# VectorE's weight splits moved ahead of the S5 set-up in the first mixer of a two-layer decoder trunk

## What is computed

```python
for l in range(DEPTH):                       # 2 layers, 256 tokens, width 1024
    h = rms_norm(x, mix_norm[l])
    z = h @ w_in[l]                          # 1024 -> 5632 columns
    u, q, k, v, g_ssm, g_attn = jnp.split(z, SPLITS, axis=-1)
    y_a = s5_branch(u, ...)                  # diagonal complex state space model, 32 groups x 64 states
    y_a = jax.nn.gelu(y_a)
    y_a = y_a * jax.nn.sigmoid(y_a @ w_glu[l] + b_glu[l])
    q, k = apply_rope(q), apply_rope(k)      # per 64-wide component
    y_b = diff_attention(q, k, v, lam)       # 8 heads, two maps each, then a norm per head
    m = sigmoid(g_ssm) * (y_a @ w_proj_ssm[l]) + sigmoid(g_attn) * (y_b @ w_proj_attn[l])
    x = x + m @ w_out[l]
    x = x + FFN(rms_norm(x, ffn_norm[l]))    # layer 0 dense, layer 1 top-2 of 8 experts
return rms_norm(x, final_norm)
```

## Time and profile before

| what | value |
|---|---|
| median of three runs | 1532.93 us |
| the profiled execution | 1532.64 us, of which the span of the trace is 1530.9 us |
| TensorE busy in the span | 1489.4 us (97%) |
| VectorE, ScalarE, GpSimd busy | 1214.7, 901.7 and 72.8 us |
| bytes moved by DMA | 393.07 MB, mean 257 GB/s |
| mean granted TensorE clock | 0.992 of full speed |

### The profile page before, as it was taken

One profiled execution on the slowest core, in us unless ns is written; L12 is line 12 of the kernel. 1 busy time (PEld: TensorE's weight loads), 2 busy tenths in 40 slices (PEclk: granted clock), 3 DMA queues, 4 the chain that ended last, 5 costly groups with the idle time before them and its releaser, 6 DMA issues.

```text
span 1530.9 us, 23739 instructions
## 1 busy us (share of the span) xinstructions
PE 1489.4 (97%) x8995; PEld 1262.2 (82%) x8995; DVE 1214.7 (79%) x1291; ACT 901.7 (59%) x882; POOL 72.8 (5%) x115
## 2 busy tenths in 40 slices
PE   7999999999999999997999999999999999999997
PEld 5788888999998888886888888888888888888886
DVE  7897876565466787857988879889888798888986
ACT  5244654344334346634777767667677677776775
POOL 2900100000000001000000000000000000000000
PEclk9899999999999999999999999999999999999999
DMA  6444443554344434352988998989989899899894
GB/s 246 152 144 142 148 175 155 208 191 166 122 182 179 182 134 152 143 197 100 399 342 328 383 344 317 369 321 360 364 323 371 329 362 343 326 385 343 314 362 168
DMA packets 76929, 393.07 MB, mean 257 GB/s; under 512 B 28225, under 2 KB 28353, under 8 KB 30018
## 3 DMA queue, kind: packets, MB, share of 16 engines
q1 hardware_dynamic: 75392, 391.28, 67.7%
q10 hardware_dynamic: 1474, 0.91, 0.2%
HBM read 388.36 MB, written 1.05 MB: 254 GB/s over the span
## 4 chain that ended last, share of the span: by engine, by line
PE 81%; DVE 7%; SPq 3%; ACT 3%; issue 3%; DMA 2%; DVEq 0%; ACTq 0%; POOL 0%; POOLq 0%
PE psum L1690 25%; PE psum L1692 24%; PE psum L1691 24%; PE psum L1706 3%; SPq L647 3%; DVE w_lo L561 2%; DMA w_raw<-in_stream 2%; PE psum L1998 2%; ACT w_hi L555 2%; PE psum L1712 1%; SPq L656 1%; PE psum L1804 1%; PE psum L1741 1%; PE psum L2016 0%; PE psum L2017 0%
## 5 line engine op out<-in xcount | busy, mean ns | idle before, releaser
L561 DVE TENSOR_TENSOR w_lo<-w_raw,w_hi 128x2048 fp32r<-128x2048 f32 x270 | 614.2, 2290 | 157.1 <-ACT w_hi L555 155.8
L555 ACT ACTIVATE w_hi<-w_raw 128x2048 fp32r<-128x2048 f32 x270 | 513.7, 1913 | 292.4 <-PE psum L1692 249.0
L1690 PE MATMUL psum<-w_hi,hsT_hi 128*128 128x512 f32 (+1 forms) x512 | 187.8, 367 | 1.6 <-issue 1.6
L1692 PE MATMUL psum<-w_lo,hsT_hi 128*128 128x512 f32 (+1 forms) x512 | 186.1, 364 | 0.0
L1691 PE MATMUL psum<-w_hi,hsT_lo 128*128 128x512 f32 (+1 forms) x512 | 186.0, 363 | 0.0
L1690 PE MATMUL psum<-w_hi,hT_hi 128*128 128x512 f32 x384 | 156.0, 406 | 4.9 <-DVE w_lo L561 4.7
L1691 PE MATMUL psum<-w_hi,hT_lo 128*128 128x512 f32 x384 | 152.0, 396 | 0.0
L1692 PE MATMUL psum<-w_lo,hT_hi 128*128 128x512 f32 x384 | 151.8, 395 | 0.0
L561 DVE TENSOR_TENSOR w_lo_more<-w_raw,w_hi_more 128x2048 fp32r<-128x2048 f32 x56 | 128.0, 2286 | 26.2 <-ACT w_hi_more L555 26.2
L1690 PE MATMUL psum<-hT_hi,w_hi 128*128 128x256 f32 x416 | 119.1, 286 | 3.0 <-DVE hT_lo L1233 2.0
L555 ACT ACTIVATE w_hi_more<-w_raw 128x2048 fp32r<-128x2048 f32 x56 | 107.0, 1911 | 20.1 <-DMA w_raw<-in_stream 13.3
(11 more groups left out here) (387 smaller groups left out, 2760.1 us busy)
## 6 DMA issues: line engine op xcount, KB each, us to landing
w_raw<-in_stream SPq DMA_DIRECT2D x326, 1024.0 KB, 6.6
w_raw_more<-in_stream SPq DMA_DIRECT2D x40, 1024.0 KB, 7.3
gain_row<-in_gain_rows SPq DMA_DIRECT2D x3, 512.0 KB
x_tok<-in_x SPq DMA_DIRECT2D x1, 1024.0 KB, 5.1
uT_lags<-uT_by_lag SPq DMA_DIRECT2D x64, 16.0 KB, 1.9
zT_by_lag<-uT_lags SPq DMA_DIRECT2D x64, 16.0 KB, 1.8
out_trunk<-out_tok SPq DMA_DIRECT2D x2, 512.0 KB, 2.6
s_direct<-s_direct_lags SPq DMA_DIRECT2D x40, 16.0 KB, 2.0
```

The source lines that it names most:

```text
L555: nc.scalar.activation(split_of(seg, i)[0], raw_of(seg, i), ACT.Copy).then_inc(s_hi, 1)
L561: nc.vector.tensor_tensor(l_, raw_of(seg, i), h.bitcast(F32), ALU.subtract).then_inc(s_lo, 1)
L1690: mm(out, lh, rh, start=start, stop=False)
L1692: return mm(out, lh, rl, start=False, stop=stop)
```

## The change

Five edits, all in the first mixer's pass of VectorE and in what belongs to it:

```diff
-SETUP_MID = {5: [("bT", 2), ("bT", 3)]}
-SETUP_TAIL = {4: [("bT", 0), ("bT", 1)], 5: [("tT", 0)]}
+SETUP_MID = {6: [("bT", 2), ("bT", 3)]}
+SETUP_TAIL = {5: [("bT", 0), ("bT", 1)], 7: [("tT", 0)]}
...
-        Bl = [at(f"s5_b_powers{l}", [P, 2, PAIRS, LAGS, GCH], F32, (a_q, a_k)[l]) for l in range(DEPTH)]
+        Bl = [at(f"s5_b_powers{l}", [P, 2, PAIRS, LAGS, GCH], F32, (a_v, a_k)[l]) for l in range(DEPTH)]
...
-        Craw = at("s5_c_raw", [P, 2, PAIRS, GCH], F32, a_att)
+        Craw = at("s5_c_raw", [P, 2, PAIRS, GCH], F32, a_yl)
...
                 fr, fi = (flat(a).rearrange("p (o n) -> p o n", o=1).to_broadcast([P, LAGS, DEPTH * PAIRS])
                           for a in (s5fr, s5fi))
+                split_ahead(dve_split, dve, 0, 1)
...
-                own.do(V.tensor_tensor(x1, x1, x2, ALU.add))
-                own.settle()
-                V.tensor_scalar(Ein[:, :, 1:LAGS + 1, :], x1, -1.0, None, ALU.mult).then_inc(s_e, 1)
+                x1, x2 = (a.rearrange("p q d n -> p q (d n)") for a in (x1, x2))
+                V.scalar_tensor_tensor(Ein[:, :, 1:LAGS + 1, :].rearrange("p q d n -> p q (d n)"), x1, -1.0, x2,
+                                       ALU.mult, ALU.subtract).then_inc(s_e, 1)
...
-                    if l == 0 and s < 5:
+                    if l == 0 and s in (0, 2, 3, 4):
                         split_ahead(dve_split, dve, seg, s)
                     if l == 0 and s == 0:
                         constants()
-                    if l == 0 and s == 1:
-                        b_powers(0, 0)
-                    if l == 0 and s == 2:
-                        b_powers(0, 1)
                     if l == 0 and s in (2, 3):
-                        c_powers(0, s - 2)
+                        b_powers(0, s - 2)
...
                     if s < SEG - 1 and (l or s >= 5):
                         split_ahead(dve_split, dve, seg, s)
+                    if l == 0 and s == 5:
+                        c_powers(0, 0)
+                        c_powers(0, 1)
```

## The result

| kernel | median of runs | lowest to highest | profiled execution | span | mean granted clock |
|---|---|---|---|---|---|
| before | 1531.32 us (20 runs) | 1528.89 to 1535.15 | 1532.64 us | 1530.9 us | 0.992 |
| after | 1535.86 us (20 runs) | 1533.53 to 1539.24 | 1535.83 us | 1533.8 us | 0.991 |

The ratio after to before is 1.0028, 95% interval 1.0021 to 1.0035: 4.3 us slower by the ratio. The forecast was 1530.5 us (1527.0 to 1534.0), 2.3 us faster for the profiled execution.

A forecast was written before the change was run, and what follows sets the result against it. TensorE bounds the kernel (81% of the chain); its two waits cost 8.3 us, of which about 6 go back to a new wait. 1532.64 - 2.3 = 1530.3, stated as 1530.5 us, range 1527 to 1534.

The forecast's parts named there:

- The waits before slots 3 and 5 go, with their half clock: TensorE's two waits for VectorE's split vanish, 4.7 us, with the half-clock stretches behind them, 3.6 us: 8.3 us.
- The powers then take 5.2 + 4.9 - 2.1 + 1.3 = 9.3 and end at 67.0 (66.5 to 67.8): VectorE's powers of C, moved behind the split of slot 7, with add and negation fused, take 9.3 us.
- tT takes 4.3: TensorE's tT, after slot 7, takes 4.3 us as in the old trace and ends at 71.7.
- The end of the copy at 72.15: ScalarE's copy of tT's result, behind slot 10's high part, ends at 72.15 us; before, it ended at 68.4.
- SP's 20 issues: SP issues the 20 shift_direct DMAs behind tT's copy one by one, in 12.7 to 14.6 us.
- the wait of 6.3 to 8.2: VectorE asks for the 20 copies at 80.6 and stands still 6.3 to 8.2 us before the states' last two instructions.
- 14.64 + 1.8 from slot 10 to 12: TensorE from slot 10 to slot 12: the old 14.64 us plus 1.8 for one half-clock stretch, bounds 0 and 3.6.
- The fused instruction: In C's powers, add and negation (1.34 and 0.80 us) become one VectorE instruction of 1.3 us, bounds 0.8 and 2.1.
- Rival B: Slower: late DMA issues and half clock behind both TensorE idles, or slipping C's powers or copy; 1534 us, chance 0.12.
- A: Rival: the new wait for the copies does not bind, slot 10 starts about 88.2; 1524 us, chance 0.11.
- C: Rival: VectorE bounds from slot 10 on, its gelu waits staying in full; 1531.6 us, chance 0.17.
- Everything behind moves by the same amount: From slot 12 on VectorE catches up, so all later work shifts as slot 12 does: 1.4 to 3.3 us earlier.

The follow-up runs named there:

- x1: Changed kernel with GpSimd's six doublings of the table of turns replaced by a memset (output differs): 1532.16 us, ratio 1.0004 to the kernel before.
- x2: Changed kernel with 40 idle products on TensorE ahead of tT's wait for C's powers: 1533.40 us, ratio 1.0009 to the kernel before.
- x3: Changed kernel with the 20 copies' source in its own memory, so VectorE need not wait for them: 1530.66 us, ratio 0.9995 to the kernel before.
- x7: Changed kernel with the add and negation of C's powers as two instructions again: 1540.74 us, ratio 1.0054 to the kernel before.
- x8: Changed kernel with 10 of the 20 copies issued by ScalarE and 40 idle products before tT: 1528.83 us, ratio 0.9974 to the kernel before.
- x4: Changed kernel with 10 of the 20 copies behind tT issued by ScalarE, first mixer only: 1532.66 us, ratio 1.0002 to the kernel before.
- x9: Changed kernel with idle products before tT, the copies' source in its own memory, and half the copies issued by ScalarE: 1526.96 us, ratio 0.9965.
- x10: Kernel before, with separate copy source, half the copies issued by ScalarE, and 40 idle products before waits in slots 3 and 5: 1532.61 us, ratio 1.0005.

## Why the prediction was wrong

- **The waits before slots 3 and 5 go, with their half clock: right.** Slots 3 to 7 started within 0.3 us of the forecast (slot 4 at 40.26 for 40.1, slot 7 at 62.20 for 61.9).
- **VectorE's line to 57.7: right** (57.84).
- **"The powers then take 5.2 + 4.9 - 2.1 + 1.3 = 9.3 and end at 67.0 (66.5 to 67.8)": this step failed.** It took the durations from the place where the powers stood (1.34 for the add) and moved them. In the new place GpSimd's doublings are 256 and 496 elements wide, not 32 to 128, and VectorE's wide instructions took 1.57 to 1.95 us, where they had taken 1.24 to 1.43 in the old place and take 1.22 without GpSimd: 12.0 us for the whole. The prediction asked what the move does to GpSimd (would the turns be late?) and not what GpSimd does to VectorE. Its rows had a hint: the split at 65.69 took 2.71 instead of 2.29, beside GpSimd's wide work. Without GpSimd the powers take 8.4 (x1), and 3.7 us of time come back.
- **"tT takes 4.3": failed as a consequence.** With 2.2 us of idling ahead of it, it ran at 1.2 GHz, 6.7 us. The prediction charged the half clock for the waits that it foresaw, and had none here. By x2 this is 2.4 us.
- **The end of the copy at 72.15: 77.40.** The difference of 5.2 is 2.6 us of `tT`'s start, 2.4 of its length and 0.2 from its end to that of the copy.
- **SP's 20 issues (12.7 to 14.6 less the landing), the landing, the wait of 6.3 to 8.2, 5.3 us from release to the split of slot 10: right**, each within its bounds (13.3; 2.0; 7.84; 92.82 to 98.1). x3 shows that the wait is what costs: without it 5.0 us come back. The 2.0 us of the landing came from the rows. (The Trainium skill's page "DMA: Bandwidth & Descriptors", section "Anatomy of one DMA", which the prediction names beside them, gives its 2.0 us for DMAs issued by GpSimd; here SP issues them.)
- **14.64 + 1.8 from slot 10 to 12: 16.2 in the profile** (114.44 less 98.22), so 1.6 for 1.8; but 17.4 in the second profile and 17.5 in x1, 2.8 and 2.9 over, within the bound of 3.6.
- **The fused instruction: 1.3 taken, 1.95 measured, 1.22 without GpSimd.** Within the bounds of 0.8 to 2.1. x7 shows that it earned its place.
- **Rival B** had the time (1533.3 to 1536) and, as a way there, a slip of C's powers and of the copy; it was given 0.12 and a slip of 1 to 2 us. The slip was 5.2. Of its two conditions one came (the last copy landed after 89.5, at 92.7); the other, the clock low past slot 11, did not (low from 98.5 to 101.9). So its time came out mostly by a larger slip than it named. A, which needs no binding wait, and C, VectorE as the bound, did not come: VectorE's split of slot 12 was done at 113.6, before TensorE took it at 114.4.
- **"Everything behind moves by the same amount", from slot 12 on: only roughly.** By its splits and high parts, the changed kernel's first profile is about 3 us late from there to 247, 4.6 behind the low stretch at 262, 3.0 from about 407 (the kernel before has a low stretch at 399 that this one lacks), 6.1 from 438 (TensorE waits 1.84 us at 428.70 where the kernel before waits 0.19, with a low stretch behind it), and 3.2 at 1440. Other kernels have or lack such stretches there as well. The sign and the size of the loss therefore rest on the 20 runs of each kernel and not on this one profile. Why the clock falls in one execution and not in another stays open.

On VectorE and GpSimd the Trainium skill's page "SBUF — State Buffer", section "SBUF: two separate sides", says that the two share a pair of ports that one instruction holds exclusively until its end, a VectorE instruction with two inputs in SBUF against a GpSimd instruction that reads it. The rows agree that the two hold each other up, but with less than the whole duration: GpSimd's 128x496 takes 1.05 us with VectorE mostly out of its way, and VectorE's instruction between two of them takes 1.95 instead of 1.22; for 128x256 it is 0.66, and 1.65 instead of 1.22. The added time, 0.35 to 0.55 beside 128x256 and 0.73 beside 128x496, is GpSimd's own duration less 0.1 to 0.3 us. An estimate by the rule, with GpSimd's whole duration added to each, four instructions beside 0.66 and two beside 1.05, gives 4.7 us on top of the forecast's 67.0, so an end between 67.0 and 71.7; it was 69.9. That sum was missing. That the ports are the reason is the page's account; the runs show that the delay goes when GpSimd's work goes (x1).

## What to carry to other kernels

An instruction's duration belongs to the place where it was measured: before moving VectorE work, read what GpSimd does in the new place and how wide. A wait that is moved onto a chain of many small DMAs can be met at the chain (two queues gave 4.0 us, a source that nobody has to wait for gave 5.0). The 2.2 us of idling before small matmuls cost 2.4 more in clock, which 40 idle products kept away. Where a change is lost to a new wait, repair the wait before dropping the change: here the change went from 0.28% slower to, with three repairs, 0.35% faster.

## What the runs showed of the hardware

- Beside VectorE, GpSimd instructions of 16 to 64 elements pay and VectorE hardly does: in the changed kernel GpSimd's 128x16 product took 2.39 us beside a split of 2.29, alone about 0.26, and VectorE's wide instructions in the kernel before stay at 1.23 to 1.35 instead of 1.22. Wider ones cost both: beside 128x128 VectorE takes 1.34 to 1.43 (kernel before, 54 to 58 us), beside 128x256 1.57 to 1.77, beside 128x496 1.95. Even a small VectorE instruction can be caught: L1140 took 1.12 us instead of 0.28 beside GpSimd's copy of 1024 elements.
- A VectorE instruction of two inputs and a scalar on 1024 elements takes 1.22 us, the same as a plain one of two inputs (both in x1).
- The clock, once low behind or in an idle of about 2.2 us, stayed low for 10.2 us over `tT`'s small matmuls (71 to 81 in the changed kernel; 6.8 us in x3). Around the waits that 512-column matmuls followed it was low for 3.4 us in the kernel before (slots 3 and 5) and in the changed one (slot 10, from 98.5, 0.3 us behind the wait), and for 6.8 us in x2, x7, x8 and in the changed kernel's second profile, where it fell 0.8 to 1.8 us before the wait's end.
- Most issues of small DMAs take 0.65 us on SP and 0.65 to 0.7 on ScalarE, side by side (x4). Single ones take longer, often on both at once: 1.6 and 2.0 us in x9. So 10 took 6.5 to 8.9 us on SP and 6.8 to 10.2 on ScalarE (x4, x8, x9, x10).
- A copy of 16 KB lands 2.0 us after its issue in most cases, but the last of ScalarE's ten took 3.5, 5.6 and 5.2 us in x4, x8 and x9, each time as SP went back to loading 1 MB tiles.
